# Modulation columns made by turning the running sums and adding them up on VectorE, with the sums moved into the down projections and four local reorderings

## The reference, cut to what matters

```
def _swiglu(x, w1, w3, w2):
    return (jax.nn.silu(x @ w1) * (x @ w3)) @ w2          # 1024 -> 2816 -> 1024
...
for l in range(2):
    h = _swiglu(x, ffn_w1[l, 0], ffn_w3[l, 0], ffn_w2[l, 0])
    x = _layernorm(ALPHA * x + 0.5 * h, ln_g[l, 0], ln_b[l, 0])
    h = _mixer(x, l, ...)      # q, k, v, gates; rotary on q and k; attention; projections
    x = _layernorm(ALPHA * x + h, ln_g[l, 1], ln_b[l, 1])
    h = _swiglu(x, ffn_w1[l, 1], ffn_w3[l, 1], ffn_w2[l, 1])
    x = _layernorm(ALPHA * x + 0.5 * h, ln_g[l, 2], ln_b[l, 2])
...
mod = silu(c) @ w_mod + b_mod              # 6144 numbers: sh1, sc1, g1, sh2, sc2, g2
mod_c = silu(c_ctx) @ w_mod + b_mod        # of these sh1 and sc1 are used
h = rmsnorm(x, norm1_g) * (1 + sc1) + sh1  # second block's attention input
...
x = x + g1 * mix
h2 = rmsnorm(x, norm2_g) * (1 + sc2) + sh2
x = x + g2 * swiglu(h2, w_ffn_gate, w_ffn_up, w_ffn_down)
```

## Time and profile before

| what | value |
|---|---|
| median of 3 runs | 1716.27 us (1715.16 to 1721.95) |
| profiled execution: its own time, its span | 1717.35 us, 1715.6 us |
| PE, DVE, ACT, POOL busy share of the span | 99%, 69%, 50%, 13% |
| granted TensorE clock | 1.00 over the span |
| moved by DMA | 334.70 MB, mean 195 GB/s |

### The profile page before, as it was taken

One profiled execution on the slowest core, in us unless ns is written; L12 is line 12 of the kernel. 1 busy time (PEld: TensorE's weight loads), 2 busy tenths in 40 slices (PEclk: granted clock), 3 DMA queues, 4 the chain that ended last, 5 costly groups with the idle time before them and its releaser, 6 DMA issues.

```text
span 1715.6 us, 31006 instructions
## 1 busy us (share of the span) xinstructions
PE 1696.8 (99%) x12649; PEld 1582.4 (92%) x12649; DVE 1179.7 (69%) x1877; ACT 857.8 (50%) x1411; POOL 229.7 (13%) x293
## 2 busy tenths in 40 slices
PE   9999999999999999999999999999999999999999
PEld 8998898999899889998898999999888888999999
DVE  5674758777786667774677776777775747786653
ACT  5454454675454435453544764544536447565443
POOL 2000042211000000000132211000012515220000
PEclk9999999999999999999999999999999999999999
DMA  8676577445567647575676445777535434446753
GB/s 266 215 267 199 177 239 245 163 140 184 199 231 240 227 160 254 199 253 193 207 226 212 143 160 183 245 247 256 210 126 156 115 85 148 134 162 201 242 191 105
DMA packets 257581, 334.70 MB, mean 195 GB/s; under 512 B 15242, under 2 KB 217232, under 8 KB 257440
## 3 DMA queue, kind: packets, MB, share of 16 engines
q1 hardware_dynamic: 251312, 317.42, 55.8%
q0 software_dynamic: 6128, 15.31, 2.8%
HBM read 327.45 MB, written 1.05 MB: 191 GB/s over the span
## 4 chain that ended last, share of the span: by engine, by line
PE 79%; DVE 8%; DMA 7%; ACT 3%; issue 2%; SPq 0%; POOL 0%; DVEq 0%; POOLq 0%
PE bank L783 16%; PE bank L786 16%; PE bank L784 16%; PE bank L827 7%; PE bank L828 7%; PE bank L825 6%; DMA raw<-in_ffn_w_dram 4%; DVE wlo L2166 4%; DMA mtmp<-mtmp 3%; ACT whi L1691 2%; PE bank L978 1%; PE bank L976 1%; PE bank L1127 1%; PE bank L928 1%; PE bank L1474 1%
## 5 line engine op out<-in xcount | busy, mean ns | idle before, releaser
L2166 DVE TENSOR_TENSOR wlo<-raw,whi 128x1024 fp32r<-128x1024 f32 x549 | 669.5, 1228 | 301.1 <-ACT whi L1691 299.4
L1691 ACT ACTIVATE whi<-raw 128x1024 fp32r<-128x1024 f32 x549 | 571.0, 1052 | 375.0 <-PE bank L828 208.0
L783 PE MATMUL bank<-XTh,whi 128*128 128x256 f32 x1936 | 541.4, 280 | 0.0
L786 PE MATMUL bank<-XTh,wlo 128*128 128x256 f32 x1936 | 539.3, 279 | 1.2 <-DVE wlo L2166 1.1
L784 PE MATMUL bank<-XTl,whi 128*128 128x256 f32 x1936 | 537.6, 278 | 0.0
L786 PEld LDWEIGHTS bank<-XTh,wlo 128*128 128x128 f32 x1936 | 364.6, 188 | 3.4 <-DVE wlo L2166 2.9
L783 PEld LDWEIGHTS bank<-XTh,whi 128*128 128x128 f32 x1936 | 364.2, 188 | 1.0
L784 PEld LDWEIGHTS bank<-XTl,whi 128*128 128x128 f32 x1936 | 364.4, 188 | 0.0
L783 PE MATMUL bank<-HCh,whi 128*128 128x256 f32 (+1 forms) x832 | 236.5, 284 | 0.4 <-ACT whi L1691 0.4
L786 PE MATMUL bank<-HCh,wlo 128*128 128x256 f32 (+1 forms) x832 | 234.6, 282 | 1.1 <-DVE wlo L2166 1.1
L784 PE MATMUL bank<-HCl,whi 128*128 128x256 f32 (+1 forms) x832 | 234.4, 282 | 0.0
(11 more groups left out here) (404 smaller groups left out, 2441.3 us busy)
## 6 DMA issues: line engine op xcount, KB each, us to landing
raw<-in_ffn_w_dram SPq DMA_DIRECT2D x131, 1024.0 KB, 5.1
raw<-in_w_in_dram SPq DMA_DIRECT2D x76, 1024.0 KB, 5.1
raw<-in_w_mod_dram SPq DMA_DIRECT2D x24, 1024.0 KB, 5.1
raw<-in_w_branch_dram SPq DMA_DIRECT2D x16, 1024.0 KB, 5.0
raw<-in_w_out_dram SPq DMA_DIRECT2D x12, 1024.0 KB, 4.8
raw<-in_w_ffn_gate_dram SPq DMA_DIRECT2D x11, 1024.0 KB, 5.0
raw<-in_w_ffn_up_dram SPq DMA_DIRECT2D x11, 1024.0 KB, 5.2
raw<-in_w_ffn_down_dram SPq DMA_DIRECT2D x8, 1024.0 KB, 4.9
```

The costliest lines, as they stand in the source:

```text
L783: e.matmul(o, hi[:, k, w0:w0 + nc_], xh, start=first and k == 0, stop=False)
L786: m = e.matmul(o, lo[:, k, w0:w0 + nc_], xh, start=False, stop=last and k == nk - 1)
L1691: e.activation(in_copies(n, hi_part(n)), raw_part(n), ACTF.Copy).then_inc(WHI.did(n), 1)
L2166: e.tensor_tensor(in_copies(n, lo_part(n)), raw_part(n), in_copies(n, hi_part(n)).bitcast(F32), ALU.subtract).then_inc(WLO.did(n), 1)
```

## The change

The modulation columns of all groups but the last (g = 11) are made in another way. PE now transposes the sum, four 128 by 128 blocks for each sum, into a PSUM bank of its own (`sum_columns` on PE), and DVE adds up each of the four blocks along its free axis into 4 columns (one `tensor_reduce` of 128x512 for each sum, `sum_columns` on DVE). `settle` falls away with it. Where a group has one sum, its second column stays at the zero that POOL wrote at the start.

The table `MODS` is thinned, and six halves move behind chunks of the down projections (`DOWN_MODS`). The calls for seven groups move to fixed places between parts of the down projections (`DOWN_COLUMNS`: after which part, which group): g0 and g8 in i = 0, g3 and g5 in i = 1, g1 and g7 in i = 2, g9 in i = 3. At the norms stand g4 (j = 0), g6 (j = 2), g2 (j = 3, two sums) and g10 (j = 5). The sums of the first three stages get five buffers in place of two.

Four reorderings come with it. In the rotary, `times_sin` and `add_parts` stand three steps behind the product, and the statistics of V one step later. The first two q products are multiplied as a pair (all high products of both first). In `layernorm(2)` the columns come behind `low_x(3, 0, 1)`. At the entry of the last feed-forward, ACT and DVE split one part each earlier, and both h come before both low parts. The last two output blocks are turned, copied and stored one by one.

```diff
-        {4: (1, 3, 0), 8: (1, 3, 1), 14: (1, 4, 0), 16: (1, 4, 1), 18: (1, 7, 0), 20: (1, 7, 1)},
-        {4: (2, 1, 0), 8: (2, 1, 1), 14: (2, 2, 0), 18: (2, 2, 1)},
+        {4: (1, 3, 0), 8: (1, 3, 1), 12: (1, 5, 0), 16: (1, 5, 1)},
+        {4: (2, 1, 0), 8: (2, 1, 1), 12: (2, 7, 0), 16: (2, 7, 1)},
...
-AT_NORM = {0: 8, 2: 7, 3: 2, 5: 10}
+DOWN_MODS = ({4: (0, 4, 0), 10: (0, 4, 1)}, {4: (1, 6, 0), 10: (1, 6, 1)}, {4: (2, 2, 0), 10: (2, 2, 1)}, {})
+DOWN_COLUMNS = ({3: 0, 8: 8}, {3: 3, 8: 5}, {3: 1, 8: 7}, {2: 9})
+SUM_OF = {0: (0, 1), 8: (2,), 4: (3,), 3: (0, 1), 5: (2,), 6: (3,), 1: (0, 1), 7: (2,), 2: (3, 4), 9: (0,), 10: (1,), 11: (0,)}
+AT_NORM = {0: 4, 2: 6, 3: 2, 5: 10}
...
+            def sum_columns(g, i, b):                      # on PE
+                q.wait_ge(DMD, ("sums", g))
+                for m, a in enumerate(SUM_OF[g]):
+                    empty(b + m)
+                    for j in range(4):
+                        o = e.transpose(bank[b + m][:, j * 128:(j + 1) * 128], SUMS[i][a][:, j * 128:(j + 1) * 128], ident)
+                    emptied[b + m] = ((DMD, ("columns", g, m)),)
+                o.then_inc(MOD.did(("columns", g)), 1)
...
+            def sum_columns(g, b):                         # on DVE
+                q.wait_ge(MOD, ("columns", g))
+                q.wait_ge(PST, "modc")
+                for m in range(len(SUM_OF[g])):
+                    e.tensor_reduce(modc[:, 4 * g:4 * g + 4, m], bank[b + m][:, :].rearrange("p (j c) -> p j c", j=4), AX.X, ALU.add)...
...
-                    if n > 1:
-                        times_sin(n - 2)
+                    if n > 2:
+                        times_sin(n - 3)
                     if n:
                         times_cos(n - 1)
-                    if n > 1:
-                        add_parts(n - 2)
+                    if n > 2:
+                        add_parts(n - 3)
...
-                    if i in (2, 4):
+                    if i in (3, 5):
                         stats_v(i // 2 - 1)
-                    if i in (3, 5):
-                        norm_v(i // 2 - 1)
+                    if i in (4, 6):
+                        norm_v(i // 2 - 2)
...
                     gemm_a(bank[b][:, 0:T], xt, ("qk", l, n))      # PE, now for n > 1
+                    if n == 0:
+                        empty(1)
+                        gemm_pair([bank[i][:, 0:T] for i in range(2)], xt, names=[("qk", l, i) for i in range(2)])
...
-                finish(3)
+                for m in (6, 7):
+                    b = m - 4
+                    q.wait_ge(D2, ("out", m))
+                    empty(b)
+                    for t in range(2):
+                        r = e.transpose(bank[b][:, t * 128:(t + 1) * 128], tmp[...]...)
+                    r.then_inc(TURN.did(("last", m)), 1)
```

More of the change, by code:

```diff
@@ L233, in plan_ffn @@
                 chunk_b(w2, k, 2, 0, 1024, STANDS)
+                if k in down_mods:
+                    on_dve[len(chunks)] = down_mods[k]
+                    plan_mod(down_mods[k][1], (4 * down_mods[k][2],))
         else:
@@ L497, in program @@
             ffn1 = ffn_bufs(st, "ffn1")
-            sums1 = some(st, "sums1", 2, [128, 512])
+            sums1 = some(st, "sums1", 5, [128, 512])
         with ExitStack() as st:
@@ L647, in program @@
         for m in range(8):
-            t2r.use(("out", m), (TURN, ("out", m // 2)))
+            t2r.use(("out", m), (TURN, ("out", m // 2) if m < 6 else ("last", m)))
         def chunk_here(q, c, j=None):
@@ L745, in sync @@
             store(2)
-            store(3)
-            q.wait_ge(STORED, 3)
+            for m in (6, 7):
+                q.wait_ge(A2, ("last", m))
+                e.dma_start(out[0, :, m * 128:(m + 1) * 128].rearrange("(t p) c -> p t c", p=128),
+                            OUT[:, :, m * 128:(m + 1) * 128]).then_inc(STORED.did(("last", m), by=16), 16)
+            q.wait_ge(STORED, ("last", 7))
         def tensor(e):
@@ L954, in ffn_mods @@
                 for f, (_, g, h) in MODS[i].items():
-                    if h and g not in AT_NORM.values():
+                    if h and i == 4:
                         at[f + 2] = lambda g=g: modulation(g, i, mod_bank(i))
@@ L1012, in turn_first, with ffn_down, between @@
                 emptied[0] = ((DFF, ("hl", i, 1)),)
-            def ffn_down(i, between=None):
+            def ffn_down(i, context=None):
                 Hh, Hl = FFN[i][0:2]
+                calls = [0]
+                def between():
+                    calls[0] += 1
+                    if calls[0] in DOWN_COLUMNS[i]:
+                        g = DOWN_COLUMNS[i][calls[0]]
+                        sum_columns(g, i, 4 - len(SUM_OF[g]))
+                    if context:
+                        context()
                 def ready(k, t):
@@ L1067, in mixer @@
                     if k == 1:
[L1068 removed]
+                        sum_columns(AT_NORM[3 * l], 2 * l, 6)
                 value("x low", 0, 0)
@@ L1652, in second @@
                             finish(c - 1)
-                finish(3)
+                for m in (6, 7):
+                    b = m - 4
+                    q.wait_ge(D2, ("out", m))
+                    empty(b)
+                    for t in range(2):
+                        r = e.transpose(bank[b][:, t * 128:(t + 1) * 128], tmp[t2r.slot["out", m]][:, t * 128:(t + 1) * 128], ident)
+                    r.then_inc(TURN.did(("last", m)), 1)
             def warm(k):
@@ L2124, in second @@
                     w.give_back()
+                w.more(1)
                 for j in range(2):
@@ L2138, in second @@
                                          ACTF.Copy).then_inc(A2.did(("out", c - 1)), 1)
-                q.wait_ge(TURN, ("out", 3))
-                e.activation(OUT[:, :, 768:1024], bank[3][:, :].rearrange("p (t c) -> p t c", t=2), ACTF.Copy).then_inc(A2.did(("out", 3)), 1)
+                for m in (6, 7):
+                    q.wait_ge(TURN, ("last", m))
+                    e.activation(OUT[:, :, m * 128:(m + 1) * 128], bank[m - 4][:, 0:T].rearrange("p (t c) -> p t c", t=2), ACTF.Copy).then_inc(
+                        A2.did(("last", m)), 1)
             for t in range(2):
@@ L2192, in low_x, with down_columns, between @@
                                 hi.bitcast(F32), ALU.subtract).then_inc(XLO.did(("x", s, t, c)), 1)
+            def sum_columns(g, b):
+                q.wait_ge(MOD, ("columns", g))
+                q.wait_ge(PST, "modc")
+                for m in range(len(SUM_OF[g])):
+                    e.tensor_reduce(modc[:, 4 * g:4 * g + 4, m], bank[b + m][:, :].rearrange("p (j c) -> p j c", j=4), AX.X, ALU.add).then_inc(
+                        DMD.did(("columns", g, m), g), 1)
+            def down_columns(i, context=None):
+                calls = [0]
+                def between():
+                    calls[0] += 1
+                    if calls[0] in DOWN_COLUMNS[i]:
+                        g = DOWN_COLUMNS[i][calls[0]]
+                        sum_columns(g, 4 - len(SUM_OF[g]))
+                    if context:
+                        context()
+                return between
             def mod_columns(g, b):
@@ L2285, in layernorm @@
                 scale(1)
-                if j in AT_NORM and turn:
-                    mod_columns(AT_NORM[j], 3 if j == 2 else 6)
+                if j % 3 == 0:
+                    sum_columns(AT_NORM[j], 6)
                 if j % 3 and turn:
                     low_x(j + 1, 0, 1)
+                if j == 2:
+                    sum_columns(AT_NORM[j], 3)
+                if j % 3 and turn:
                     w.more(1)
@@ L2808, in second @@
                 w.take()
+                w.give_back()
                 for k in range(4, 8):
                     low_h2(k)
+                w.take()
+                w.give_back()
                 for j in range(2):
@@ L2814, in second @@
                     scaled(2 + j, Hf[j])
-                w.give_back()
-                w.take()
-                w.give_back()
+                w.more(1)
                 for j in range(2):
@@ L2822, in second @@
                         DFF.did(("h", 4, j)), 1)
+                for j in range(2):
                     q.wait_ge(AFF, ("hh", 4, j))
```

49 lines of the change are left out of this document (27 added, 22 removed), and 2 rows, old and new, of the table MODS.

## The result

The changed kernel takes 1695.1 us in the median of 4 runs (1694.39 to 1696.64), beside 1718.09 for the kernel before in the same series (1715.16 to 1721.95, 4 runs). The ratio is 0.9866, with a 95% interval of 0.9843 to 0.9889. A second series, with 4 and 7 runs, gave 1695.13 beside 1715.79, ratio 0.9880 (0.9857 to 0.9904). The profiled pair has spans of 1715.6 and 1692.7 us, 22.9 less; the forecast's sum was 15.5.

What follows compares the result with a forecast made beforehand. PE, busy 99% of the span, was taken as the bound. Columns −6.3, modulation chunks −4.9, new waits +0.2, rotary −2.3, entry −1.8, end −0.4 sum to −15.5 us: 1700.8 us against the median 1716.27, range 1697 to 1706.

Steps and rivals of the forecast that it cites:

- The columns: Modulation columns on PE: transposes in place of products make groups with two sums 0.97 cheaper, one sum 0.51; 6.3 us less.
- the norm at j = 3: Group g2, two sums: PE is late there by more than the saving, so all 0.97 us counts.
- the three others: Columns at j = 0, j = 2 and the second block's entry: about 0.2, 0.1 and 0.1 us less.
- The Trainium skill's figure for a transpose: Rival for the columns: some 275 ns per 128×128 transpose, so the new form adds 3.4 us; 1710.5 us, chance 0.04.
- the six chunks: Rival in the down projections: moved modulation chunks hold buffers and PE waits for a load each; 1724.8 us, chance 0.03.
- The waits at `val`, at the entry and for `ffn1Hf`: PE's waits at the second mixer's V, last feed-forward's entry and stage i = 1's down projection: 2.3, 1.8, 2.5 us less.
- the term for stage i = 3: Fewer modulation chunks among the weight loads there end PE's waits for late low weights and h; 2.4 us less.
- The lower bound of the step: Modulation chunks, stages i = 1 and 3: only 2 us of the 4.9 gained if DVE, not DMA, makes h late.
- a larger gain: Rival: regular unlisted short waits at each down projection shrink with even loads, 3 to 4 us more; 1697 us, chance 0.06.
- The term for the rotary: Later use of the DMA copy and later scaling of V remove PE's two low-weight waits; 2.3 us less, bounds 0.3 to 2.5.
- The end: Last outputs: two transposes fewer and a half-width last copy on the final chain; 0.4 us less, bounds 0.2 to 0.8.

Runs made afterwards that it cites:

- short_sums3: Kernel before, all loads kept, seven of eight rows of each modulation sum in stage i = 3 added on only 64 of 512 columns; 1714.18 us (1 run).
- no_rotary: Changed kernel with the rotary's order put back as before; 1698.47 us (1 run).
- mods_only: Changed kernel without the hunks on the rotary, the q pair, the last feed-forward's entry and the last outputs; 1702.64 us, ratio 0.9925 to the kernel before.
- orders_only: Kernel before with only the hunks on the rotary, q pair, last feed-forward's entry and last outputs; 1708.77 us, ratio 0.9965.

## Why the prediction was right in its sign and wrong in its size

**Right, with its numbers.** PE bound the kernel. The columns were worth 5.9 us (6.3 forecast), the transposes 0.79 and 0.36, the reduction 0.684 (0.69), the norm at j = 3 gave 0.87 (0.97) and the three others 0, 0.07 and 0 (0.2, 0.1, 0.1): at j = 0 PE was earlier by the forecast's 0.5 and then waited for ACT's high weight, not for DVE. The Trainium skill's figure for a transpose (page "TensorE: Matmul & The Clock Gate", section "🔬 Part 4: PE-mode transpose") was no price here. The down projections took the six chunks with no wait. The waits at `val`, at the entry and for `ffn1Hf` went with the sizes forecast, within 0.4 us each.

**Wrong: the term for stage i = 3, size and cause.** The step reads "the weights come late, so do the splits, and DVE ... makes h late", and priced what the list of waits names, 2.4 us. The loss was 5.6, and 3.5 to 5.3 in the four other profiles that have it. The list of waits leaves out many short ones, of 0.1 us or so, which PE took at low weights and at the products behind them before the wait for h. The window over the stage had it (1017 instructions in 120 us, 27 of them for columns, where the changed kernel has 1045 and none for columns), and the price could have been taken from the stage's time against stage i = 2 of the same trace: 5.5. And the loads weren't the cause: `short_sums3` kept them and lost 0.2 us. The change helped because it halved DVE's sums in that stage. The lower bound of the step, "h stays late because DVE, not the DMA, was the cause", had the right cause and the wrong consequence, since fewer chunks also mean less for DVE. The rival "a larger gain" (0.06, 1697) came nearest to the time; it too looked for unlisted short waits, but in the down projections, and they stood in the up projection of stage i = 3.

**Missing: what follows a wait or comes by chance.** The products' rhythm gave 3.7 us net in the profiled pair, of which 1.7 at the start and 3.05 in the last up projection for the changed kernel and 1.4 in stage 0 against it. No part of the change was shown to make that; the profile of before happened to have both, its repeat had neither, so this part of the 22.9 is luck of the pair. The forecast took one profile's waits for the kernel's own. The kernel before scatters, from 1708.3 to 1724.2 over all series, and its waits bring further losses in some executions: the 1.6 to 2.0 us at `val` in four of five profiles, and the drop of the clock behind the wait for `ffn1Hf` in four of five. The timed runs fit this. In 28 of the 39 runs of the kernel before whose granted clock is on record, it is below 1.000 over the whole run (0.997 to 0.999); the 11 at 1.000 average 1712.9 us and the three at 0.997 average 1721.2. The changed kernel's eight runs are all at 1.000 and lie within 1693.1 to 1696.6. So taking the waits away most likely removed also what they drew after them, and that part of the median's gain was not in the sum. How much of the 20.7 to 23.0 us between the medians each of them makes can't be told from so few profiles.

**The term for the rotary** came out (2.2), but the reordering wasn't alone in it. With evened loads the old order lost 0.4 us in `no_rotary` and nothing in `mods_only`; with the old loads it lost 1.6 to 2.0 in four of five profiles, and the one profile with the new order there (`orders_only`) has no such wait. Two profiles and one are few: that the reordering makes sure of what the loads made likely isn't shown beyond them.

**The end** gave 0.7 for 0.4. The last copy took 0.38 us (0.45 was taken). The last stores, of 128 KB, landed in 1.8 us and those of 256 KB in 2.1 (median; 2.3 before), so half the bytes saved little. The fixed 2 us that the prediction quotes are stated by the Trainium skill (page "DMA: Bandwidth & Descriptors", section "🔬 Anatomy of one DMA — SWDGE (gpsimd) path") for transfers that GpSimd issues; SP issues these, and the small saving fits.

## What to carry to other kernels

Where an engine adds work inside a stage that it must also feed, price the stage's whole time against an undisturbed one, not the listed waits: the short ones add up to more. Before calling a load pattern the cause, take the feeding engine's work away and leave the loads. And take a second profile of the same kernel before pricing differences under 5 us: two readings of it differed by 5.8 us in span, and the loss in stage i = 3 alone by 1.9.

## What the runs showed of the hardware

- The 256-column f32 products started 113.3 or 117.7 ns apart, steadily, at a granted clock of 1.00, for some 1100 products, with 219 GB/s of DMA beside either. Each of the two groups of four 128x128 transposes in each mixer was followed by the other rhythm in all sixteen profiles, in both directions; a single transpose in one of four places.
- A wait of PE of 2.0 us was followed in four of five profiles by products at half speed (0.43 for 0.23 us, granted clock 0.50) for 2.6 to 4.7 us, and in one by none. Such a drop also followed a wait of 1.9 us (in one of four profiles that have one of 1.6 to 2.0 at that place) and one of 0.7 us.
- Eight 128x128 f32 transposes between 512-column products held them up by 0.79 us, 0.1 each; a 128x512 reduction from PSUM into 4 columns took DVE 0.68 us.
